# A sparse expert layer in fp32: the two halves of a small place's down sums are added by VectorE, and GpSimd multiplies by the share

## Chip, core and metric

One Trainium2 chip, one of its cores. The metric is the device time of one execution in microseconds (us), as the median of several runs. The engines are TensorE (PE; PEld is its loading of stationary operands), VectorE (DVE), ScalarE (ACT), GpSimd (POOL) and SyncE (SP), which issues the large loads. Matmuls write to PSUM, eight banks of 128 partitions x 512 floats; the other engines read them there.

## What is computed

A residual block: three token mixers (differential attention, an mLSTM, cross-attention), and then a sparse expert network. The change lies in the last:

```python
top_v, top_i = lax.top_k(logits, TOP_K)          # 512 tokens, 32 experts, top 4
h = lax.ragged_dot(xs, w_gate_up, group_sizes) + b_gate_up[e_sorted]
gate, up = h[:, :D_FF], h[:, D_FF:]               # D_MODEL = D_FF = 1024
a = (up + 1.0) * (gate * jax.nn.sigmoid(SWIGLU_ALPHA * gate))   # both clamped
y = lax.ragged_dot(a, w_down, group_sizes) + b_down[e_sorted]
y = y * top_w.reshape(-1)[order][:, None]         # the token's share
out = jax.ops.segment_sum(y, tok, num_segments=T)
```

All in float32. The kernel reaches that precision by splitting operands in two rounded parts, hi and lo, and adding the products hi·hi, hi·lo and lo·hi.

## The kernel before

**Places.** The experts are sorted by their number of tokens and seated in 32 places, 0 to 31. Places 0, 2, 4, ..., 30 and 31 are large (up to 128 tokens), places 1, 3, ..., 29 are small (up to 64, `NS`). The expert part, `stage_moe`, handles place 0, then 15 pairs (`PAIRS`) of a small and a large place in a hardware loop (the last pair is written out again behind it), then place 31. A pass over one place is a `turn`; an odd turn is `turn(..., cur=1, prev=0)`, an even one `turn(..., cur=0, prev=1)`.

**Units.** The weights of an expert come in 12 units of 1 MB: 0 to 3 and 8 to 11 are gate and up, 4 to 7 are down. SyncE loads a unit again as soon as TensorE has used the last one in its place (`s_use`). ScalarE copies it to a rounded hi (`hi`, line 2213, moe_hi, a ring of 6), VectorE subtracts to get lo (`lo`, line 2220, moe_lo), and TensorE multiplies. These two are the splits. ScalarE runs 5 units ahead of TensorE, VectorE 4; the position in a turn is called a slot, 0 to 11, and each engine's queue is an order written out by hand, slot by slot.

**A turn.** TensorE's turn n multiplies tokens of place n with the units 0 to 3 (banks Hb), turns the activations of place n-1 (`turn_a`, line 2306), multiplies those of place n-1 with the down units 4 to 7 (banks Yb[0] and Yb[1]), turns the first half of the activations of n, goes on with the units 8 and 9, transposes the tokens of place n+1 (`turn_x`, line 2248) into the same two banks Yb, and ends with the units 10 and 11. VectorE makes the activations (`swiglu`, lines 2363 and 2369) and the lo parts of activations (`keep_a_lo`, lines 2385 and 2388) and tokens (`keep_x_lo`, lines 2343 and 2345); ScalarE the hi parts (`keep_a_hi`, line 2378, moe_aTh).

**Small places.** In a small place the stationary operand has the hi parts of 64 tokens in columns 0 to 63 and their lo parts in columns 64 to 127, so that two matmuls do for three (lines 2230 and 2231). The result stands in two halves of a bank, partitions 0 to 63 and 64 to 127, that must be added. For this ScalarE copies the bank to SBUF (`to_fold`, line 2278, moe_fold), and TensorE multiplies it with the 128 x 64 matrix `onto`, two identities one above the other, back to partitions 0 to 63 of the bank (`fold_down`, line 2272; one such fp32 matmul is two records). A small place takes six folds: four for gate and up, two for its down sums, Yb[0] and Yb[1], which fall into the even turn.

**The result y.** ScalarE multiplies each half of y (512 columns) by the token's share and writes it to SBUF (`weigh`, line 2399, moe_y). The second half lets two others go on: `turn_x` of TensorE waits for `s_ys` before it overwrites the banks, and GpSimd adds the rows of y to the output with an indirect DMA (`late`, line 2435). GpSimd's queue holds per turn: the gather of the tokens of place n+1 (`fetch`, line 2414), the bias row of n+1, and `late` for place n-1, which first copies the list of tokens and shares to moe_LS (line 2404).

```python
if not (isinstance(n, int) and n < 2):
    pe.wait_ge(s_ys, n * 2 - 2)          # in turn_x
```

Of the kernel before, what the change touches and what calls it, by code (L numbers as in the profile page):

```python
# [27 lines left out]
F32 = mybir.dt.float32  # L28
# [7 lines left out]
P = 128  # L36
# [2103 lines left out]
def stage_moe(K, ctx):  # L2140
# [15 lines left out]
    LS, LO_list = (sb(n, [P, 4], I32) for n in ("LS", "LO"))  # L2156
    Hb, Yb, Tb = K.banks[0:4], K.banks[4:6], K.banks[6:8]
    (s_hi, s_lo, s_use, s_LS, s_XT, s_XTh, s_XTl, s_sel, s_sg, s_cl, s_a, s_aT, s_aTh, s_aTl,
     s_ys, s_sc, s_LO, s_bd, s_h1, s_fk, s_fd, s_fc) = (K.sem("moe_" + n) for n in (
         "unit_hi", "unit_lo", "unit_used", "list_late", "XT", "XT_hi", "XT_lo", "bias_row",  # L2160
         "silu", "up_clipped", "a", "aT", "aT_hi", "aT_lo", "y", "scattered", "over_list", "bias_down", "h1", "to_fold", "folded", "fold_const"))
    CAPPED = ALPHA * LIMIT / (1.0 + math.exp(-ALPHA * LIMIT))
    DOWN = range(4, 8)
    B = 12 * NE + 4
# [103 lines left out]
    def fold_down(pe, f, bank):  # L2268

        pe.wait_ge(s_fc, 1)  # L2270
        pe.wait_ge(s_fk, f + 1)
        nc.tensor.matmul(bank[0:NS, :], onto[:], fold[:], start=True, stop=True).then_inc(s_fd, 1)  # L2272

    def to_fold(act, f, bank, ready):

        act.wait_ge(s_use, ready)
        act.wait_ge(s_fd, f + 1)
        nc.scalar.activation(fold[:], bank[:], ACT.Copy).then_inc(s_fk, 1)
# [109 lines left out]
        nc.vector.scalar_tensor_tensor(aTl[:, cols], Tb[half][:], 1.0 / ALPHA, aTh[:, cols].bitcast(F32), ALU.mult,  # L2388
                                       ALU.subtract).then_inc(s_aTl, 1)

    def weigh(act, n, j, ready, small=0):

        act.wait_ge(s_fd if small else s_use, ready)
        rows = NS if small else P
        if j == (1 if isinstance(n, int) and n == NE - 1 else 0):
            act.wait_ge(s_LS, n + 1)
            if not (isinstance(n, int) and n == 0):
                act.wait_ge(s_sc, n * 16)
        nc.scalar.activation(y[0:rows, j * 512:(j + 1) * 512], Yb[j][0:rows, :], ACT.Copy,  # L2399
                             scale=LS[:].bitcast(F32)[0:rows, 2:3]).then_inc(s_ys, 1)  # L2400

    def entry(pool, dst, kept, n, entries):

# [21 lines left out]
            return  # L2425
        nc.gpsimd.tensor_copy(sel[par][:], K.moe_pick[:, ds(e, 1)].broadcast_to([P, P])).then_inc(s_sel, 1)

    def late(pool, n, entries, small=0):

        rows = NS if small else P  # L2430
        if not (isinstance(n, int) and n == 0):
            hold(K, pool, s_sc, n * 16)
        entry(pool, LS, s_LS, n, entries)
        hold(K, pool, s_ys, n * 2 + 2)
        nc.gpsimd.indirect_dma_start(A["out"], bass.IndirectOffsetOnAxis(ap=LS[0:rows, 0:1], axis=0), y[0:rows, :], None,  # L2435
                                     bounds_check=S - 1, oob_is_err=False, compute_op=ALU.add).then_inc(s_sc, 16)

# [8 lines left out]

    def pair(it, turn, last=0):

        turn(it * 2 + 1, 1, True, 1, 0, 0, it * 6)
        turn(it * 2 + 2, 0, True, 0, 1, 1 - last, None, it * 6)  # L2450

    with nc.Block(no_gpsimd_drain=True) as block:
        @block.sync
# [28 lines left out]

        @block.tensor
        def _(pe):
            def turn(n, par, more, cur=0, prev=0, nxt=0, f=None, g=None):
# [24 lines left out]
                if cur:  # L2510
                    fold_down(pe, f + 1, Hb[1])
                pe.wait_ge(s_aTl, START + n * 2)
                downs(5)
                downs(6)
                if prev:
                    fold_down(pe, g + 4, Yb[0])
                downs(7)
                turn_a(pe, n, 0)
                ups(2, 0)
                if prev:  # L2520
                    fold_down(pe, g + 5, Yb[1])
# [41 lines left out]
        def _(act):  # L2563
# [7 lines left out]
                else:  # L2571
                    hi(act, n + 1, slot - 7)

            def turn(n, par, more, cur=0, prev=0, nxt=0, f=None, g=None):
                for slot in range(12):
                    if slot == 0 and prev:
                        to_fold(act, g + 3, Hb[3], n * 12)
# [9 lines left out]
                        to_fold(act, f + 1, Hb[1], count(n, 3))  # L2587
                    if prev:
                        if slot == 6:
                            to_fold(act, g + 4, Yb[0], count(n, 5))  # L2590
                        if slot == 7:
                            weigh(act, n - 1, 0, g + 6, 1)
                        if slot == 8:
                            to_fold(act, g + 5, Yb[1], count(n, 7))
                        if slot == 9:
                            weigh(act, n - 1, 1, g + 7, 1)
                    else:
                        if slot == 6:
# [61 lines left out]
        def _(pool):  # L2660
# [11 lines left out]
            def turn(n, par, more, cur=0, prev=0, nxt=0, f=None, g=None):  # L2672
# [5 lines left out]
                late(pool, n - 1, listed(expert(pool, n - 1)), prev)  # L2678

            def list_over():  # L2680

# [38 lines left out]
        def _(dve):  # L2720
# [4 lines left out]
                else:  # L2725
                    lo(dve, n + 1, slot - 8)

            def turn(n, par, more, cur=0, prev=0, nxt=0, f=None, g=None):
                for slot in range(12):
                    if slot == (1 if prev else 0):  # L2730
                        swiglu(dve, n - 1, 1, g + 5 if prev else n * 12, prev)
                    if slot == (3 if prev else 2):
                        keep_a_lo(dve, n - 1, 1, prev)
                    if slot == (6 if cur else 4):
                        swiglu(dve, n, 0, f + 3 if cur else count(n, 3), cur)
                    if slot == 8:
# [241 lines left out]
```

## Time and profile before

| | us |
|---|---|
| median of 3 runs | 2204.12 (2203.06 to 2205.08) |
| the profiled execution | 2202.52 |
| its span, first to last instruction | 2200.9 |
| of it the expert part, from the first moe split | from about 1082 on |
| TensorE busy | 2137.9 (97%) |
| VectorE busy | 1562.1 (71%) |
| ScalarE busy | 1323.6 (60%) |
| GpSimd busy | 400.3 (18%) |

All numbers of a view come from one profiled execution; times in it run from the start of its span. Busy shares are means over the span. In the timeline a row is an instruction or a run of the same instruction; "idle before" is how long its engine had nothing to do, with the instruction that ended the wait. The ends of matmuls are modelled and overlap the next start, so the distance between starts is what a matmul costs.

### The profile page before, as it was taken

The numbers are of one execution on the slowest core, as the hardware profiler recorded it, in microseconds if no ns is written. First come the engines' busy times: TensorE is split into PE (matmuls) and PEld (weight loads), VectorE is DVE, ScalarE is ACT, GpSimd is POOL, SyncE is SP. The second block draws the span as 40 slices with busy tenths as digits, with TensorE's granted clock in tenths as the row PEclk, the third lists the DMA queues.
The fourth block names the chain that finished last, engine by engine and source line by source line (L and its number), as shares of the span: only waits on it lengthen the run. The fifth ranks groups of instructions, "written<-read, shape, count | busy, mean of one in ns | idle before, by whom it ended". The sixth has DMA issues, their size and how long they took to land.

```text
span 2200.9 us, 29939 instructions
## 1 busy us (share of the span) xinstructions
PE 2137.9 (97%) x9668; PEld 1656.9 (75%) x9668; DVE 1562.1 (71%) x1706; ACT 1323.6 (60%) x1618; POOL 400.3 (18%) x414
## 2 busy tenths in 40 slices
PE   6999899999999999999799999999999999999998
PEld 6888677776676888888567777777777777777776
DVE  6777444754434334335689999999999999999986
ACT  5565443443323433223268888888888888888884
POOL 3333100201221000001112213212122121121210
PEclk9999999999999999999689999999999999999999
DMA  4110332421112344334579999999999999999993
GB/s 191 58 57 29 102 113 73 145 64 39 38 48 97 95 136 139 97 96 158 210 303 380 390 391 382 396 388 378 396 385 386 392 382 392 380 384 397 382 382 122
DMA packets 87143, 515.76 MB, mean 234 GB/s; under 512 B 13236, under 2 KB 14260, under 8 KB 36312
## 3 DMA queue, kind: packets, MB, share of 16 engines
q1 hardware_dynamic: 79496, 498.06, 59.2%
q0 software_dynamic: 7296, 16.79, 3.4%
q8 instruction: 37, 0.61, 0.1%
q14 instruction: 26, 0.21, 0.0%
q10 hardware_dynamic: 288, 0.09, 0.0%
HBM read 504.66 MB, written 19.40 MB: 238 GB/s over the span
## 4 chain that ended last, share of the span: by engine, by line
PE 50%; DVE 1%; ACT 0%; issue 0%; POOL 0%; POOLq 0%; DVEq 0%; ACTq 0%
PE bank L2237 9%; PE bank L2239 8%; PE bank L2238 8%; PE bank L2230 8%; PE bank L2231 7%; PE bank L2272 4%; PE bank L2259 1%; PE bank L2248 1%; PE bank L2306 1%; PE bank L2290 0%; DVE moe_lo L2220 0%; ACT moe_hi L2213 0%; POOL out L2435 0%; DVE moe_a L2369 0%; DVE moe_um L2363 0%
## 5 line engine op out<-in xcount | busy, mean ns | idle before, releaser
L2220 DVE TENSOR_TENSOR moe_lo<-moe_raw,moe_hi 128x2048 fp32r<-128x2048 f32 x382 | 855.5, 2285 | 11.0 <-ACT moe_hi L2213 9.4
L2213 ACT ACTIVATE moe_hi<-moe_raw 128x2048 fp32r<-128x2048 f32 x380 | 723.5, 1914 | 73.7 <-PE bank L2239 65.8
L173 ACT ACTIVATE unit_hi<-unit_raw 128x1024 fp32r<-128x1024 f32 x116 | 122.2, 1060 | 238.5 <-DMA unit_raw<-in_w_units 232.4
L179 DVE TENSOR_TENSOR unit_lo<-unit_raw,unit_hi 128x1024 fp32r<-128x1024 f32 x116 | 146.5, 1268 | 160.9 <-ACT unit_hi L173 160.5
L2435 POOL DMA_INDIRECT out<-moe_y,moe_LS x32 | 109.8, 3431 | 684.8 <-ACT moe_y L2399 684.8
L2237 PE MATMUL bank<-moe_hi,moe_XTh 128*128 128x512 f32 x544 | 218.9, 402 | 0.0
L2239 PE MATMUL bank<-moe_hi,moe_XTl 128*128 128x512 f32 x544 | 214.3, 394 | 0.0
L2238 PE MATMUL bank<-moe_lo,moe_XTh 128*128 128x512 f32 x544 | 214.0, 393 | 0.0
L2230 PE MATMUL bank<-moe_hi,moe_XTh 128*128 128x512 f32 x480 | 193.3, 403 | 0.0
L2231 PE MATMUL bank<-moe_lo,moe_XTh 128*128 128x512 f32 x480 | 189.8, 395 | 0.0
L2237 PEld LDWEIGHTS bank<-moe_hi,moe_XTh 128*128 128x128 f32 x544 | 103.4, 190 | 43.9 <-issue 24.3
L2230 PEld LDWEIGHTS bank<-moe_hi,moe_XTh 128*128 128x128 f32 x480 | 90.7, 189 | 42.9 <-issue 23.5
L2239 PEld LDWEIGHTS bank<-moe_hi,moe_XTl 128*128 128x128 f32 x544 | 103.0, 189 | 23.1
L2238 PEld LDWEIGHTS bank<-moe_lo,moe_XTh 128*128 128x128 f32 x544 | 103.1, 190 | 21.2
L2237 PE MATMUL bank<-moe_hi,moe_aTh 128*128 128x512 f32 x272 | 107.8, 396 | 0.6 <-DVE moe_lo L2220 0.6
L2239 PE MATMUL bank<-moe_hi,moe_aTl 128*128 128x512 f32 x272 | 106.1, 390 | 0.0
L2238 PE MATMUL bank<-moe_lo,moe_aTh 128*128 128x512 f32 x272 | 105.9, 389 | 0.0
L2231 PEld LDWEIGHTS bank<-moe_lo,moe_XTh 128*128 128x128 f32 x480 | 90.4, 188 | 20.5
L1741 PE MATMUL bank<-yH,unit_hi 128*128 128x512 f32 x256 | 99.8, 390 | 2.2 <-DVE mix_da_lo L1640 2.2
L1743 PE MATMUL bank<-yH,unit_lo 128*128 128x512 f32 x256 | 99.9, 390 | 0.0
L393 PE MATMUL bank<-da_slab_hi,xnH 128*128 128x384 f32 x256 | 92.3, 361 | 5.0 <-DVE xnL L214 5.0
L2272 PE MATMUL bank<-moe_fold,moe_onto 128*64 128x512 f32 x180 | 96.5, 618 | 0.0
(395 smaller groups left out, 4349.5 us busy)
## 6 DMA issues: line engine op xcount, KB each, us to landing
moe_raw<-in_w_moe SPq DMA_DIRECT2D x384, 1024.0 KB, 7.6
unit_raw<-in_w_units SPq DMA_DIRECT2D x116, 512.0 KB, 3.6
da_slab<-in_w_qkv SPq DMA_DIRECT2D x8, 1536.0 KB, 6.6
y_caT<-in_x SPq DMA_DIRECT2D x4, 512.0 KB, 6.1
yda_d<-y_daT SPq DMA_DIRECT2D x1, 2048.0 KB, 6.3
y_daT<-in_blocks_qk SPq DMA_DIRECT2D x1, 2048.0 KB, 10.5
y_daT<-yda_d SPq DMA_DIRECT2D x1, 2048.0 KB, 8.1
y_daT<-in_x SPq DMA_DIRECT2D x1, 2048.0 KB, 8.6
```

The source lines that it names most:

```text
L173: K.nc.scalar.activation(K.whi[:, i, :], K.wraw[:, i, :], ACT.Copy).then_inc(K.s_whi, 1)
L179: K.nc.vector.tensor_tensor(K.wlo[:, i, :], K.wraw[:, i, :], K.whi[:, i, :].bitcast(F32), ALU.subtract).then_inc(K.s_wlo, 1)
L1743: mm = nc.tensor.matmul(bank[:], wl, hi[:, x], start=False, stop=(k0 + k == depth - 1))
L2213: nc.scalar.activation(HI[ring(n, pos)][:], RAW[pos][:], ACT.Copy).then_inc(s_hi, 1)
L2220: nc.vector.tensor_tensor(LO[pos][:], RAW[pos][:], HI[ring(n, pos)][:].bitcast(F32), ALU.subtract).then_inc(s_lo, 1)
L2230: nc.tensor.matmul(bank[:], xh[:, x], HI[ring][:, w], start=start and k == 0, stop=False)
L2231: mm = nc.tensor.matmul(bank[:], xh[:, x], LO[pos][:, w], start=False, stop=stop and k == 3)
L2237: nc.tensor.matmul(bank[:], xh[:, x], HI[ring][:, w], start=start and k == 0, stop=False)
L2238: nc.tensor.matmul(bank[:], xh[:, x], LO[pos][:, w], start=False, stop=False)
L2239: mm = nc.tensor.matmul(bank[:], xl[:, x], HI[ring][:, w], start=False, stop=stop and k == 3)
L2272: nc.tensor.matmul(bank[0:NS, :], onto[:], fold[:], start=True, stop=True).then_inc(s_fd, 1)
L2435: nc.gpsimd.indirect_dma_start(A["out"], bass.IndirectOffsetOnAxis(ap=LS[0:rows, 0:1], axis=0), y[0:rows, :], None, bounds_check=S - 1, oo ...
```

## The change

The folds of the two down sums go. For a small place ScalarE now copies only the lower half of the bank, partitions 64 to 127, to partitions 0 to 63 of y (`keep_rest`, slots 6 and 8 of the even turn). VectorE adds the upper half out of PSUM (`add_rest`, slots 7 and 9, ahead of that slot's split). GpSimd multiplies the whole of y, 64 x 1024, by the share before its indirect DMA. The semaphore `s_ys`, for which `turn_x` waits, is now raised by VectorE for a small place. Large places are as before. In a pair four folds remain; the counts of folds in the loop go from `it * 6` to `it * 4`.

```diff
+    def keep_rest(act, n, j, ready):
+
+        act.wait_ge(s_use, ready)
+        if j == 0:
+            act.wait_ge(s_sc, n * 16)
+        nc.scalar.activation(y[0:NS, j * 512:(j + 1) * 512], Yb[j][NS:P, :], ACT.Copy).then_inc(s_yt, 1)
+
+    def add_rest(dve, j, kept):
+
+        dve.wait_ge(s_yt, kept)
+        cols = y[0:NS, j * 512:(j + 1) * 512]
+        nc.vector.tensor_tensor(cols, Yb[j][0:NS, :], cols, ALU.add).then_inc(s_ys, 1)
...
         entry(pool, LS, s_LS, n, entries)
         hold(K, pool, s_ys, n * 2 + 2)
+        if small:
+            nc.gpsimd.tensor_scalar(y[0:NS, :], y[0:NS, :], LS[0:NS, 2:3].bitcast(F32), None, ALU.mult).then_inc(s_yw, 1)
+            hold(K, pool, s_yw, w)
...
                 downs(5)
                 downs(6)
-                if prev:
-                    fold_down(pe, g + 4, Yb[0])
                 downs(7)
                 turn_a(pe, n, 0)
                 ups(2, 0)
-                if prev:
-                    fold_down(pe, g + 5, Yb[1])
                 ups(2, 1)
...
                     if prev:
                         if slot == 6:
-                            to_fold(act, g + 4, Yb[0], count(n, 5))
-                        if slot == 7:
-                            weigh(act, n - 1, 0, g + 6, 1)
+                            keep_rest(act, n - 1, 0, count(n, 5))
                         if slot == 8:
-                            to_fold(act, g + 5, Yb[1], count(n, 7))
-                        if slot == 9:
-                            weigh(act, n - 1, 1, g + 7, 1)
+                            keep_rest(act, n - 1, 1, count(n, 7))
...
+                    if slot == 7 and prev:
+                        add_rest(dve, 0, it * 2 + 1)
                     if slot == 8:
                         keep_a_lo(dve, n, 0, cur)
+                    if slot == 9 and prev:
+                        add_rest(dve, 1, it * 2 + 2)
```

VectorE in the even turn, from the split of unit 10 to the lo parts of the next place's tokens, in the kernel before:

```order
L2220 TENSOR_TENSOR moe_lo_5680<-moe_raw_5668,moe_hi_5686 128x2048
L2219 REGISTER_ALU
L2220 TENSOR_TENSOR moe_lo_5681<-moe_raw_5669,moe_hi_5687 128x2048
L2388 SCALAR_TENSOR_TENSOR moe_aTl<-bank,moe_aTh 128x512
L2219 ISA
L2220 TENSOR_TENSOR moe_lo_5670<-moe_raw_5658,moe_hi_5682 128x2048
L2219 REGISTER_ALU
L2220 TENSOR_TENSOR moe_lo_5671<-moe_raw_5659,moe_hi_5683 128x2048
L2339 REGISTER_ALU
L2343 TENSOR_TENSOR moe_XTh_8208<-bank,moe_XTh_8208 128x4x64 x2
```

and in the changed one:

```order
L2220 TENSOR_TENSOR moe_lo_5680<-moe_raw_5668,moe_hi_5686 128x2048
L2402 TENSOR_TENSOR moe_y<-bank,moe_y 64x512
L2219 REGISTER_ALU
L2220 TENSOR_TENSOR moe_lo_5681<-moe_raw_5669,moe_hi_5687 128x2048
L2388 SCALAR_TENSOR_TENSOR moe_aTl<-bank,moe_aTh 128x512
L2219 ISA
L2220 TENSOR_TENSOR moe_lo_5670<-moe_raw_5658,moe_hi_5682 128x2048
L2402 TENSOR_TENSOR moe_y<-bank,moe_y 64x512
L2219 REGISTER_ALU
L2220 TENSOR_TENSOR moe_lo_5671<-moe_raw_5659,moe_hi_5683 128x2048
L2339 REGISTER_ALU
L2343 TENSOR_TENSOR moe_XTh_8208<-bank,moe_XTh_8208 128x4x64 x2
```

The second addition stands behind the split of the next place's unit 0 (moe_lo_5670) and ahead of that of unit 1.

TensorE in the same turn, at the first of the two folds, between the down units 6 and 7 (the difference, - before, + changed):

```order
 L2230 MATMUL bank<-moe_hi_5682,moe_aTh 128x512
 L2231 MATMUL bank<-moe_lo_5676,moe_aTh 128x512
-L2271 REGISTER_ALU
-L2272 MATMUL bank<-moe_fold,moe_onto 64x512
 L2225 REGISTER_ALU
 L2230 MATMUL bank<-moe_hi_5683,moe_aTh 128x512
```

The matmuls of units 6 and 7 now follow each other; nothing else moves on TensorE.

## Rows read from the trace of the kernel before

**Rows 1.** The page, busy time of an engine, share of the span, instructions

```profile
PE 2137.9 (97%) x9668; PEld 1656.9 (75%) x9668; DVE 1562.1 (71%) x1706; ACT 1323.6 (60%) x1618; POOL 400.3 (18%) x414
```

**Rows 2.** Window of one pair: PE, PEld, DVE, ACT, POOL busy; clock, DMA share, GB/s

```profile
1562.62:1630.29 67.67, 67.67 (x295) 50.47 (x293) 62.24 (x41) 55.77 (x47) 14.62 (x12) 1.00 1.00 389
```

**Rows 3.** Timeline of TensorE at the first removed fold: start, length, line, operation

```profile
1586.81 0.39 PE L2231 MATMUL bank<-moe_lo,moe_aTh 128*128 128x512 f32 x1
1587.13 1.07 PE L2272 MATMUL bank<-moe_fold,moe_onto 128*64 128x512 f32 x2
1588.13 0.50 PE L2230 MATMUL bank<-moe_hi,moe_aTh 128*128 128x512 f32 x1
```

**Rows 4.** Timeline of TensorE: transposes of a, and of the next tokens

```profile
1578.39 0.60 PE L2306 MATMUL bank<-ident,moe_a 128*128 128x128 f32 x4
...
1597.25 0.39 PE L2239 MATMUL bank<-moe_hi,moe_XTl 128*128 128x512 f32 x1
...
1597.48 1.03 PE L2248 MATMUL bank<-ident,moe_Xg 128*128 128x128 f32 x8
```

**Rows 5.** Timeline of VectorE, same turn, and one row of the next; idle in brackets

```profile
1572.67 0.68 DVE L2363 TENSOR_SCALAR moe_um<-bank 64x512 f32<-64x512 f32 x1
...
1580.80 0.42 DVE L2385 SCALAR_TENSOR_TENSOR moe_aTh<-bank,moe_aTh 128x256 fp32r<-128x256 f32 x1 [2.33 <-ACT moe_aTh L2378]
...
1583.34 0.69 DVE L2363 TENSOR_SCALAR moe_um<-bank 128x512 f32<-128x512 f32 x1
...
1584.67 8.89 DVE L2220 TENSOR_TENSOR moe_lo<-moe_raw,moe_hi 128x2048 fp32r<-128x2048 f32 x4
...
1593.48 0.68 DVE L2388 SCALAR_TENSOR_TENSOR moe_aTl<-bank,moe_aTh 128x512 fp32r<-128x512 f32 x1
...
1594.08 4.48 DVE L2220 TENSOR_TENSOR moe_lo<-moe_raw,moe_hi 128x2048 fp32r<-128x2048 f32 x2
...
1599.32 0.76 DVE L2343 TENSOR_TENSOR moe_XTh<-bank,moe_XTh 128x256 fp32r<-128x256 f32 x2 [0.76 <-ACT moe_XTh L2333]
...
1626.92 0.42 DVE L2385 SCALAR_TENSOR_TENSOR moe_aTh<-bank,moe_aTh 128x256 fp32r<-128x256 f32 x1 [1.54 <-ACT moe_aTh L2378]
```

**Rows 6.** Timeline of ScalarE in the same turn

```profile
1578.59 1.92 ACT L2213 ACTIVATE moe_hi<-moe_raw 128x2048 fp32r<-128x2048 f32 x1 [0.47 <-PE bank L2239]
...
1580.40 0.37 ACT L2378 ACTIVATE moe_aTh<-bank 128x256 fp32r<-128x256 f32 x1
...
1594.72 0.69 ACT L2399 ACTIVATE moe_y<-bank,moe_LS 64x512 f32<-64x512 f32 x1 [1.23 <-PE bank L2272]
```

**Rows 7.** Timelines of TensorE and VectorE at two restarts, and windows around them

```profile
696.14 0.47 PE L1741 MATMUL bank<-yH,unit_hi 128*128 128x512 f32 x1 [2.16 <-DVE mix_da_lo L1640]
696.44 0.39 PE L1742 MATMUL bank<-mix_da_lo,unit_hi 128*128 128x512 f32 x1
...
1132.11 0.69 DVE L2369 SCALAR_TENSOR_TENSOR moe_a<-moe_sg,moe_um 128x512 f32<-128x512 f32 x1
1132.86 1.12 PE L2306 MATMUL bank<-ident,moe_a 128*128 128x128 f32 x4 [3.15 <-DVE moe_a L2369]
...
694.00:700.00 6.00, 3.86 (x17) 3.22 (x18) 4.70 (x8) 5.34 (x9) 0.00 (x0) 1.00 0.31 87
1133.00:1137.00 4.00, 4.00 (x14) 3.06 (x14) 4.00 (x2) 3.52 (x4) 0.00 (x0) 0.62 0.69 283
```

**Rows 8.** Lines and DMA: durations ns min/median/max, and us from issue to landing

```profile
L285 POOL TENSOR_SCALAR ropeS<-ropeS x2: 305/305/305, 19.1 to 21.2; 128x128 f32<-128x128 f32 x2
...
L2404 POOL COPY moe_LS<-first x32: 184/414/5111, 1127.1 to 2176.7; 128x4 int32 x32
...
L2220 DVE TENSOR_TENSOR moe_lo<-moe_raw,moe_hi x348: 2275/2284/2376, 1159.9 to 2137.7; 128x2048 fp32r<-128x2048 f32 x174
...
moe_Xg<-hn_d,moe_LG POOLq DMA_INDIRECT x26, 10.4
```

**Rows 9.** Window with the lowest DMA share of six; columns as in rows 2

```profile
1586.00:1588.00 2.00, 2.00 (x8) 0.85 (x6) 2.00 (x2) 1.90 (x2) 0.00 (x0) 1.00 0.82 332
```

More of the change, by code:

```diff
@@ L2158, in stage_moe @@
     (s_hi, s_lo, s_use, s_LS, s_XT, s_XTh, s_XTl, s_sel, s_sg, s_cl, s_a, s_aT, s_aTh, s_aTl,
-     s_ys, s_sc, s_LO, s_bd, s_h1, s_fk, s_fd, s_fc) = (K.sem("moe_" + n) for n in (
+     s_ys, s_sc, s_LO, s_bd, s_h1, s_fk, s_fd, s_fc, s_yt, s_yw) = (K.sem("moe_" + n) for n in (
          "unit_hi", "unit_lo", "unit_used", "list_late", "XT", "XT_hi", "XT_lo", "bias_row",
-         "silu", "up_clipped", "a", "aT", "aT_hi", "aT_lo", "y", "scattered", "over_list", "bias_down", "h1", "to_fold", "folded", "fold_const"))
+         "silu", "up_clipped", "a", "aT", "aT_hi", "aT_lo", "y", "scattered", "over_list", "bias_down", "h1", "to_fold", "folded", "fold_const", "y_rest", "y_weighed"))
     CAPPED = ALPHA * LIMIT / (1.0 + math.exp(-ALPHA * LIMIT))
@@ L2389, in keep_a_lo, with weigh @@
                                        ALU.subtract).then_inc(s_aTl, 1)
-    def weigh(act, n, j, ready, small=0):
-        act.wait_ge(s_fd if small else s_use, ready)
-        rows = NS if small else P
+    def keep_rest(act, n, j, ready):
[7 more added lines that the diff above has]
+        nc.vector.tensor_tensor(cols, Yb[j][0:NS, :], cols, ALU.add).then_inc(s_ys, 1)
+    def weigh(act, n, j, ready):
+        act.wait_ge(s_use, ready)
         if j == (1 if isinstance(n, int) and n == NE - 1 else 0):
@@ L2398, in weigh @@
                 act.wait_ge(s_sc, n * 16)
-        nc.scalar.activation(y[0:rows, j * 512:(j + 1) * 512], Yb[j][0:rows, :], ACT.Copy,
-                             scale=LS[:].bitcast(F32)[0:rows, 2:3]).then_inc(s_ys, 1)
+        nc.scalar.activation(y[:, j * 512:(j + 1) * 512], Yb[j][:], ACT.Copy,
+                             scale=LS[:].bitcast(F32)[:, 2:3]).then_inc(s_ys, 1)
     def entry(pool, dst, kept, n, entries):
@@ L2426, in bias_row, with late @@
         nc.gpsimd.tensor_copy(sel[par][:], K.moe_pick[:, ds(e, 1)].broadcast_to([P, P])).then_inc(s_sel, 1)
-    def late(pool, n, entries, small=0):
+    def late(pool, n, entries, small=0, w=None):
         rows = NS if small else P
@@ L2447, in pair @@
     def pair(it, turn, last=0):
-        turn(it * 2 + 1, 1, True, 1, 0, 0, it * 6)
-        turn(it * 2 + 2, 0, True, 0, 1, 1 - last, None, it * 6)
+        turn(it * 2 + 1, 1, True, 1, 0, 0, it * 4)
+        turn(it * 2 + 2, 0, True, 0, 1, 1 - last, None, it * 4, it)
     with nc.Block(no_gpsimd_drain=True) as block:
@@ L2484, in _, with turn @@
         def _(pe):
-            def turn(n, par, more, cur=0, prev=0, nxt=0, f=None, g=None):
+            def turn(n, par, more, cur=0, prev=0, nxt=0, f=None, g=None, it=None):
                 def ups(j, half):
@@ L2572, in ahead, with turn @@
                     hi(act, n + 1, slot - 7)
-            def turn(n, par, more, cur=0, prev=0, nxt=0, f=None, g=None):
+            def turn(n, par, more, cur=0, prev=0, nxt=0, f=None, g=None, it=None):
                 for slot in range(12):
@@ L2670, in _, with turn @@
             nc.gpsimd.tensor_tensor(onto[:], K.ident[:, 0:NS], K.ident[:, NS:P], ALU.add).then_inc(s_fc, 1)
-            def turn(n, par, more, cur=0, prev=0, nxt=0, f=None, g=None):
+            def turn(n, par, more, cur=0, prev=0, nxt=0, f=None, g=None, it=None):
                 if more:
@@ L2677, in turn @@
                     bias_row(pool, n + 1, 1 - par, e, n * 12, nxt)
-                late(pool, n - 1, listed(expert(pool, n - 1)), prev)
+                late(pool, n - 1, listed(expert(pool, n - 1)), prev, it + 1 if prev else None)
             def list_over():
@@ L2726, in ahead, with turn @@
                     lo(dve, n + 1, slot - 8)
-            def turn(n, par, more, cur=0, prev=0, nxt=0, f=None, g=None):
+            def turn(n, par, more, cur=0, prev=0, nxt=0, f=None, g=None, it=None):
                 for slot in range(12):
```

## Prediction, made before the changed kernel ran

> **What bounds the kernel now.** I read the page first, for its busy shares: TensorE is busy for 97% of the span [rows 1]. A share is an average over stages, so the next view is the table of windows, cut to one period of the loop over pairs of places, in the expert part where the change lies. There TensorE is busy for 67.67 of 67.67 us, VectorE for 62.24, ScalarE for 55.77, and the DMA engines are at a share of 1.00 [rows 2]. The loop runs 15 times (1,015 of the 2,200.9 us), and the periods I measured differ by 0.01 us. So three resources stand within 8% of one another and TensorE is the one that never rests. What TensorE sheds is a gain only if nobody else is late where TensorE then arrives. Hence the third view: the timelines of TensorE, VectorE and ScalarE through one turn for a large place, laid over one another [rows 3 to 6].
>
> **What is removed.** A fold stands between two matmuls that start 1.32 us apart, 1586.81 and 1588.13 [rows 3]; two neighbours without one start 0.23 us apart [rows 4]. A fold costs 1.09 us of TensorE. Two of six go in each of 15 pairs: 30 × 1.09 = 32.7 us, the most that the change can give. ScalarE loses two copies and two weighings per pair and gets two copies of half height. It waited before its second weighing in this turn (1.23 us [rows 6]), so its saving is worth nothing by itself.
>
> **What is added on VectorE.** Two additions of 64 x 512 with one operand in PSUM. The nearest rows: the correction of the activations from PSUM starts at 1593.48 and the next operation at 1594.08, so such an operation shifts what follows by 0.60 us; it takes 0.68 us itself. A 64-row operation takes 0.68 us, a 128-row one 0.69 us: half height is not cheaper [rows 5]. I take 0.60 us of queue and 0.69 us to the end, with 0.1 us either way. That is 1.2 us more on an engine with 5.4 us of rest per period [rows 2]; by totals it fits. What decides is where its rest lies.
>
> **The wait that is new in kind.** TensorE's transposes of the next place's tokens go into the two banks in which the down sums stood, and wait until both halves of y are made. Before, ScalarE made them: the second from 1594.72 to 1595.41 [rows 6], and the transposes began at 1597.48 with no idle time before them [rows 4]. Now VectorE makes the second half, and its addition stands in VectorE's queue behind the splitting of the next place's unit 0. When does VectorE come there?
>
> Walk back along its queue to its last rest [rows 5]. At 1580.80 it had idled 2.33 us for ScalarE's aTh, 1580.40 to 1580.77. That stands behind a split which ScalarE began at 1578.59 when TensorE freed a ring place [rows 6]; the transposes of a, which it also needs, are at 1578.39 [rows 4]. Both are ahead of either removed fold (1587.13 and the next 6.5 us later). Nothing that is removed lets VectorE leave 1580.80 earlier, relative to TensorE's work ahead of the folds. From there it runs without rest until 1598.56: one split, two swiglu operations, four splits, the correction, two splits. The four splits take 8.89 us with 2.28 for the last, so one starts 2.20 us after another. The split of unit 0 starts at 1594.08. The first addition pushes that to 1594.68; the second addition starts at 1594.68 + 2.20 = 1596.88 and ends at 1597.57.
>
> Now TensorE. Its last matmul ahead of the transposes starts at 1597.25 and is moved forward by two folds, 2.18 us, to 1595.07; it ends at 1595.46. It then stands still for VectorE. From the end of a VectorE operation to the matmul that waited for it there are 0.06 us (1132.11 + 0.69 to 1132.86 [rows 7]): the transposes start at 1597.63, after 2.17 us of idle time. That is 0.15 us *later* than the 1597.48 of before. A matmul after such a rest costs a little more: 0.30 us to the next one instead of 0.23 [rows 7, 4], so 0.07 to 0.14 us more. **Per pair: 0.15 + 0.10 = 0.25 us longer,** since TensorE does the same as before from the transposes to the next 1578.39. Fifteen pairs: **+3.8 us**. Both ends: an addition of 0.1 us less gives +0.1 us per pair or +1.5 us in all; 0.1 us more per addition, and the dearer restart, give +0.5 us per pair or +7.5 us. The saving of 32.7 us is there, but as idle time of TensorE.
>
> **What is added on GpSimd.** One multiplication of 64 x 1024 in SBUF ahead of the scatter. No row shows one. The nearest is a tensor_scalar of 128 x 128 at 0.305 us [rows 8]; eight times as many elements are at most 2.4 us. GpSimd also gets in late: the copy of four numbers per partition takes between 0.18 and 5.11 us [rows 8]. So the scatter goes out 2 us (the later y) plus 1 to 7 us later. Behind it in GpSimd's queue stand the gather of tokens for the place after next and its bias row. TensorE transposes those tokens at the end of the next turn, some 30 us on, and a gather lands in 10.4 us [rows 8]: I cost this at nothing; the upper end is rival D.
> The Trainium skill, GPSIMD Engine Reference, section 8 (Key points), speaks against this edit: GpSimd shares its SBUF interfaces with VectorE, and contends with VectorE instructions that have two SBUF inputs. The splits are such instructions. This trace agrees on one side only: GpSimd's copies are stretched, while 348 splits lie between 2.275 and 2.376 us [rows 8]. By the rule the multiplication may also delay a split; by the rows it is GpSimd that yields.
>
> **The transfers.** With the loop 0.25 us longer they see no change: 24 loads per period, share 1.00.
>
> **Rivals.**
> *A. The adds cancel the folds (my forecast):* 2204.12 + 3.8 = 2207.9 us. Chance 0.66. Within it I give 0.47 to a change of 0.2% or less (4.4 us, about what a measurement of this kernel can tell from none) and 0.19 to more.
> *B. The stall costs TensorE its clock.* It becomes the only idle time of the loop, 2.17 us of it. For: after 3.15 us of idle time at 1132.86 the window 1133 to 1137 shows a granted clock of 0.62 of full speed [rows 7]. Against: after 2.16 us at 696.14, between dense matmuls as here, the window shows 1.00 [rows 7]. Price: a mean of 0.62 over 4 us is 3.0 us at 1.2 GHz instead of 2.4, in which half the work is lost, 1.5 us a time; in all 15 pairs 22 us, hence 2207.9 + 22 = 2230 us, and 2219 in half of them. It decides from an idle time somewhere between 2.16 and 3.15 us. Chance 0.15. The Trainium skill, TensorE: Matmul & The Clock Gate, "HAM oscillation", describes this very pattern, a gap in every step of a loop that brings half rate back each time.
> *C. VectorE comes in time.* If its place were set by TensorE's progress behind the folds, the loop would shrink by up to 2.18 us: 2171.4 us by TensorE alone. For: VectorE has 5.4 us of rest per period. Against: the rest lies at 1580.80, ahead of the additions, and nothing removed stands ahead of it. Then the DMA engines would be late next: the lowest share that I found in windows of 2 us is 0.82, from 1586 to 1588 [rows 9], 0.36 us of rest. With 0.4 to 1 us of rest per period the gain would be 6 to 15 us and whatever lead the loads have over their use: 2171 to 2198 us, I take 2185. Chance 0.11.
> *D. GpSimd holds VectorE up (slower).* The multiplication begins when the second addition is done, in the middle of splits. The additions leave VectorE 1.2 us later, TensorE 0.25. It has rests of 0.76, 1.54 and 2.33 us ahead of the next additions [rows 5]; only when GpSimd takes more than about 3.5 us from it per pair do the additions come later still. 1 us beyond that is 15 us: 2223 us. Chance 0.08.
>
> **How the numbers follow.** The profiled execution was 2202.52 us (span 2200.9), within 1.6 us of the median of 2204.12; forecast on its scale 2206.3, on the median's 2207.9. Range 2202 to 2224: A whole but for its tails (0.63), half of B (0.09), D (0.08). Left out are C and B in nearly every pair. Faster by over 0.2%: 0.11 (C). Within: 0.47. Slower: 0.19 + 0.15 + 0.08 = 0.42.
>
> **What would show it.** In the profile after: folds down from 90 to 60; a new wait of TensorE's transposes for VectorE's moe_y, 15 times at about 2.2 us, some 33 us in all; a period near 67.9 us; TensorE busy about 65.5 of it; granted clock 1.00 (B: below); GpSimd's multiplication 1 to 3 us, behind splits that stay at 2.28 us (D: stretched, or VectorE idle). I am wrong if VectorE's wait at the place of 1580.80 is gone, if the transposes wait under 1.5 us, or if ScalarE or a load is named there.

## The result, and the profile after

| | before | changed |
|---|---|---|
| median, range (7 runs each) | 2204.12 (2202.87 to 2208.07) | 2212.66 (2210.77 to 2213.82) |
| ratio, 95% interval | | 1.0038 [1.0027, 1.0049] |
| span of the profiled execution | 2200.9 | 2211.1 |

The change costs 8.5 us: slower by more than 0.2%, 4.8 us above the forecast and inside its range. The class to which the forecast gave most, a change of 0.2% or less (0.47), did not come; slower had 0.42. In the two profiled executions the spans differ by 10.2 us, of which 1.3 stand ahead of the loop's first stall, in a part that the change does not touch. TensorE did get lighter, and the time came back as a wait. (Its busy time fell by 25.5 us and not by the 36.8 of the wait, in part because work at the lower clock, shown below, takes longer.) The page, row of the engines' busy time (before: [rows 1]):

```profile
PE 2112.4 (96%) x9608; PEld 1659.9 (75%) x9608; DVE 1581.8 (72%) x1736; ACT 1304.5 (59%) x1588; POOL 519.8 (24%) x429
```

Waits of TensorE from 1160 us on: what waited for what, us in total, times, the longest. The first row has no counterpart before.

```profile
PE bank L2248 <- DVE moe_y L2402: 36.8, 15, 2.6
PE bank L2237 <- DVE moe_lo L2220: 0.6, 1, 0.6
```

The timeline of TensorE and VectorE at one of the 15 places (start, length, idle time before in brackets). VectorE first, as in [rows 5]:

```profile
1586.11 0.42 DVE L2385 SCALAR_TENSOR_TENSOR moe_aTh<-bank,moe_aTh 128x256 fp32r<-128x256 f32 x1 [2.33 <-ACT moe_aTh L2378]
...
1596.58 0.68 DVE L2402 TENSOR_TENSOR moe_y<-bank,moe_y 64x512 f32<-64x512 f32 x1
...
1599.99 2.27 DVE L2220 TENSOR_TENSOR moe_lo<-moe_raw,moe_hi 128x2048 fp32r<-128x2048 f32 x1
1602.18 0.68 DVE L2402 TENSOR_TENSOR moe_y<-bank,moe_y 64x512 f32<-64x512 f32 x1
```

And TensorE, as in [rows 4]:

```profile
1600.09 0.39 PE L2239 MATMUL bank<-moe_hi,moe_XTl 128*128 128x512 f32 x1
1602.92 1.09 PE L2248 MATMUL bank<-ident,moe_Xg 128*128 128x128 f32 x8 [2.44 <-DVE moe_y L2402]
```

VectorE's last rest before both additions is still the one of 2.33 us, with the same length and the same releaser as before. From it, everything goes in a row; the second addition ends at 1602.86 and the transposes of the next tokens begin 0.06 us later. From the rest to those transposes it was 1597.48 − 1580.80 = 16.68 us before and is 16.81 us now.

So the ordinary period grew by 0.15 us, from 67.67 [rows 2] to 67.82. But four of the 15 are longer by 1.5 to 1.6 us. Windows of an ordinary period, of a long one, and of 4 us from the stall of each kind (start and end, length, busy time of PE, PEld, DVE, ACT and POOL, granted clock, DMA share, GB/s):

```profile
1397.85:1465.67 67.82, 65.38 (x288) 50.16 (x289) 63.62 (x43) 54.52 (x44) 23.14 (x12) 1.00 1.00 388
1533.49:1602.92 69.43, 66.99 (x289) 51.53 (x289) 63.57 (x43) 54.52 (x44) 20.84 (x12) 0.98 0.98 381
1602.00:1606.00 4.00, 3.08 (x18) 2.71 (x19) 4.00 (x6) 1.87 (x3) 2.92 (x1) 1.00 1.01 422
1533.00:1537.00 4.00, 3.51 (x13) 3.18 (x14) 3.37 (x5) 1.42 (x3) 3.35 (x1) 0.57 1.01 424
```

Two equal stalls (times in which TensorE has nothing to do) of 2.44 us, one followed by TensorE at 2.4 GHz and one by a granted clock of 0.57, which is most of that stretch at 1.2 GHz. In the timeline of TensorE after the second:

```profile
1533.49 1.97 PE L2248 MATMUL bank<-ident,moe_Xg 128*128 128x128 f32 x8 [2.44 <-DVE moe_y L2402]
...
1535.68 0.63 PE L2237 MATMUL bank<-moe_hi,moe_XTh 128*128 128x512 f32 x1
...
1536.88 0.39 PE L2237 MATMUL bank<-moe_hi,moe_XTh 128*128 128x512 f32 x1
```

The eight transposes take 1.97 us, not 1.09, and the matmuls 0.63, not 0.39, until 1536.9: 3.4 us. The sum closes: 15 × 0.15 + 4 × 1.55 = 8.4 us, where 8.5 were measured. Of these only 2.2 us are the later addition; 6.2 are the clock. The four are the pairs 2, 6, 9 and 13; in two further kernels with the same stall (e6 and e10) it is four of 15 as well, the pairs 3, 6, 10 and 14, and 3, 6, 10 and 13. What picks them is open: the length of the stall does not.

GpSimd's multiplication, 15 times (duration in ns: shortest, median, longest; first and last start):

```profile
L2448 POOL TENSOR_SCALAR moe_y<-moe_y,moe_LS x15: 4707/4709/4711, 1193.1 to 2148.8; 64x1024 f32<-64x1024 f32 x15
```

### The profile page after: what moved, and what is told of

Its sections match the earlier page's. It is cut to its first block, busy times and chain, and to the rows that moved or that the text cites. A ratio compares the mean times of both kernels' runs of the same rounds, so it can differ in the third digit from the quotient of the medians.

```text
span 2211.1 us, 29775 instructions
## 1 busy us (share of the span) xinstructions
PE 2112.4 (96%) x9608; PEld 1659.9 (75%) x9608; DVE 1581.8 (72%) x1736; ACT 1304.5 (59%) x1588; POOL 519.8 (24%) x429
## 4 chain that ended last, share of the span: by engine, by line
PE 37%; DVE 9%; issue 4%; ACT 0%; DVEq 0%; POOL 0%; ACTq 0%; POOLq 0%
DVE moe_lo L2220 7%; PE bank L2237 7%; PE bank L2238 6%; PE bank L2239 6%; PE bank L2230 5%; PE bank L2231 5%; PE bank L2272 3%; PE bank L2248 2%; PE bank L2259 1%; PE bank L2306 1%; DVE moe_y L2402 1%; DVE moe_um L2363 1%; DVE moe_aTl L2388 0%; PE bank L2290 0%; ACT moe_aTh L2378 0%
## 5 line engine op out<-in xcount | busy, mean ns | idle before, releaser
L2450 POOL DMA_INDIRECT out<-moe_y,moe_LS x32 | 104.4, 3261 | 249.2 <-ACT moe_y L2411 235.6
L2448 POOL TENSOR_SCALAR moe_y<-moe_y,moe_LS 64x1024 f32<-64x1024 f32 x15 | 70.6, 4709 | 364.8 <-DVE moe_y L2402 364.8
```

## The experiments

Three questions: does the second addition's place in VectorE's queue set TensorE's start, as the forecast says; does the stall cost the clock in some pairs; and does GpSimd take anything from VectorE? The median of before was 2204.4 for e1 to e4, 2204.9 for e5 to e8, and 2206.0 for e9 and e10, each group on one chip.

### e1: the second addition one split earlier

```diff
-                    if slot == 9 and prev:
+                    if slot == 8 and prev:
                         add_rest(dve, 1, it * 2 + 2)
```

> The changed kernel with the second addition moved in VectorE's queue from slot 9 to slot 8, ahead of the split of the next place's unit 0 instead of behind it. Theory (the place of this addition in VectorE's queue ends the wait): the addition ends 2.2 us earlier relative to TensorE, the wait of the transposes falls from 2.44 us to about 0.3 us, the clock holds in all pairs, and the pair takes 67.82 - 2.1 = 65.7 us; 2212.7 - 15 x 2.1 - 4 x 1.5 = about 2175 us. Rival DMA (24 loads per pair already keep the DMA engines at a share of 1.00): TensorE's wait goes, but loads land later and later and ScalarE and TensorE come to wait for moe_raw; the pair does not go below about 67 us on the mean: 2190 to 2200 us. Rival GpSimd (the multiplication of 4.7 us holds VectorE up): less than half of the wait goes, 2200 us or more.

Measured: 2182.33 us (2179.26 to 2185.02), ratio 0.9901 [0.9888, 0.9915]. The period is 66.12 us, not the 65.7 expected. Moving one operation of 0.6 us by one split of 2.2 us is worth 30 us against the changed kernel. The waits of TensorE from 1160 us on:

```profile
PE bank L2248 <- DVE moe_y L2402: 3.7, 15, 0.4
PE bank L2306 <- DVE moe_a L2369: 3.3, 14, 0.2
```

The old wait is down to 0.24 us in 14 of 15 places and 0.39 in the last, and a second one has come up: TensorE's transposes of moe_a in the odd turn, for VectorE.

### e2: both additions in slot 7

```diff
                     if slot == 7 and prev:
                         add_rest(dve, 0, it * 2 + 1)
+                        add_rest(dve, 1, it * 2 + 2)
...
-                    if slot == 9 and prev:
-                        add_rest(dve, 1, it * 2 + 2)
```

> The changed kernel with both additions together in slot 7 of VectorE's queue, ahead of the split of unit 11. Theory: the second addition ends at about the start of what is now unit 11's split, 2 us before TensorE arrives; no wait at the transposes at all, the pair takes 65.4 us and the kernel about 2171 us, 4 us less than with slot 8. Rival DMA: as with slot 8, 2190 to 2200 us, and the two places of the addition give the same time.

Measured: 2179.29 us (2178.68 to 2181.06), ratio 0.9885 [0.987, 0.99], and a period of 66.10 us, not the 65.4 expected. The wait for moe_y is gone altogether, but the other has taken its place:

```profile
PE bank L2306 <- DVE moe_a L2369: 9.7, 14, 0.7
```

TensorE is still not alone on the path. e7 to e9 follow this up.

### e3: no sum and no multiplication

The lower halves of the small places' down sums are left out, ScalarE weighs the upper half, and GpSimd's multiplication goes.

```diff
...
-        nc.scalar.activation(y[0:NS, j * 512:(j + 1) * 512], Yb[j][NS:P, :], ACT.Copy).then_inc(s_yt, 1)
+        nc.scalar.activation(y[0:NS, j * 512:(j + 1) * 512], Yb[j][0:NS, :], ACT.Copy,
+                             scale=LS[:].bitcast(F32)[0:NS, 2:3]).then_inc(s_ys, 1)
...
-            nc.gpsimd.tensor_scalar(y[0:NS, :], y[0:NS, :], LS[0:NS, 2:3].bitcast(F32), None, ALU.mult).then_inc(s_yw, 1)
...
-                        add_rest(dve, 0, it * 2 + 1)
...
-                        add_rest(dve, 1, it * 2 + 2)
```

> The changed kernel without the two additions and without GpSimd's multiplication: ScalarE weighs partitions 0 to 63 of the down sums as they stand, and the lower halves of the down sums of small places are left out of the result. It shows what the two folds are worth alone. Theory: folds 1.2 us each, 30 of them, 36 us less than before: 2168 us, TensorE busy in all of a pair of 65.3 us. Rival DMA: 2190 to 2200 us, with waits for loads.

Measured: 2172.11 us (2171.12 to 2173.84), ratio 0.9853 [0.9838, 0.9868]. One window, and the loads issued between 1900 and 2100 us (count, size, median us from issue to landing):

```profile
1574.67:1639.87 65.20, 65.20 (x289) 50.24 (x288) 62.07 (x41) 54.51 (x45) 14.98 (x11) 1.00 1.01 400
```

```profile
moe_raw<-in_w_moe SPq DMA_DIRECT2D x74, 1024.0 KB, 17.9
```

With TensorE alone on the path a period is 65.20 us, so a fold is worth (67.67 − 65.20) / 2 = 1.23 us. The loads landed 7.7 us after their issue before and 17.9 us here, between 1900 and 2100 us: the transfers no longer keep up, but the first eleven periods are 65.20 us all the same, and only the last three are longer (65.4 to 66.2 us).

### e4: the stall filled with unread matmuls

Eight matmuls into a bank that nobody reads then, ahead of the even turn's transposes; the rest is the changed kernel.

```diff
+                if prev:
+                    for _ in range(8):
+                        nc.tensor.matmul(Tb[1][:], sel[par][:], K.moe_bias[:, 0:HF], start=True, stop=True)
```

> The changed kernel with eight matmuls of 128x512 whose result nobody reads, put on TensorE's queue ahead of the transposes of the even turn; 8 x 0.23 = 1.8 us, less than the wait of 2.44 us there. Theory (VectorE sets the start of the transposes, and the clock fell in 4 of 15 pairs because TensorE stood still): the pairs stay at 67.82 us, the wait shows as 0.6 us, the clock falls nowhere in the loop, and the time is 2204.1 + 15 x 0.15 = 2206.4 us, 6 us faster than the changed kernel in spite of more work. Rival (the fall of the clock has nothing to do with the wait, or the wait is TensorE's own cost): 2212.7 us or more, up to 2212.7 + 27 us.

Measured: 2208.06 us (2205.11 to 2210.1), ratio 1.0014 [1.0005, 1.0024]. Every period is 67.81 to 67.87 us (the last 68.02); the long ones are gone. Timeline of TensorE:

```profile
1601.67 1.09 PE L2248 MATMUL bank<-ident,moe_Xg 128*128 128x128 f32 x8 [0.57 <-DVE moe_y L2402]
```

Some 1.9 us of extra work per pair costs no time, and the kernel is 4.6 us *faster* for it (1.7 us above what was expected of it). That shows both halves of the sum: TensorE's work does not set the period, and it is the stall that brings the falls of the clock, since they go with it.

### e5: the second addition one split later

```diff
-                    if slot == 9 and prev:
-                        add_rest(dve, 1, it * 2 + 2)
                     if slot == 10:
+                        if prev:
+                            add_rest(dve, 1, it * 2 + 2)
```

(It stands ahead of the correction of the next tokens in that slot.)

> The changed kernel with VectorE's second addition one split later still (slot 10 in place of slot 9); nothing is left out. The split takes 2.20 us of the queue, so TensorE should stand idle 2.44 + 2.20 = 4.64 us ahead of the even turn's transposes. Theory (the place in VectorE's queue sets the start, and a stall this long halves the clock every time): the ordinary period goes from 67.82 to 70.0 us, and the fall of the clock adds the 1.5 us that four of fifteen pairs showed, in each pair now: 71.5 us, 15 x (71.5 - 67.67) = 57 us over the kernel before, about 2262 us. Rival (the idle time costs itself alone, and the four long pairs of the changed kernel have another cause): 70.0 us a pair, 15 x 2.35 = 35 us over, about 2240 us. If something other than VectorE's addition opened the wait, nothing moves: 2212 to 2213 us.

Measured: 2264.57 us (2264.47 to 2268.27), ratio 1.0276 [1.0261, 1.0291]; all periods are 71.66 to 71.73 us. The timeline at one stall, and the window of 4 us from there:

```profile
1697.32 1.69 PE L2248 MATMUL bank<-ident,moe_Xg 128*128 128x128 f32 x8 [4.64 <-DVE moe_y L2402]
```

```profile
1697.00:1701.00 4.00, 3.69 (x14) 3.21 (x15) 1.45 (x4) 1.88 (x3) 2.85 (x1) 0.58 0.61 252
```

The idle time is 4.64 us, as the queue's arithmetic gave, and now the clock falls every time: 71.69 = 67.82 + 2.20 + 1.67.

This run also shows GpSimd's multiplication without VectorE beside it. It starts when the second addition is done, and here VectorE then rests for over 2 us. GpSimd's line, and at the last of the 15 places the multiplication and VectorE's next operation:

```profile
L2448 POOL TENSOR_SCALAR moe_y<-moe_y,moe_LS x15: 2845/2846/2857, 1195.7 to 2199.4; 64x1024 f32<-64x1024 f32 x15
...
2199.38 2.85 POOL L2448 TENSOR_SCALAR moe_y<-moe_y,moe_LS 64x1024 f32<-64x1024 f32 x1 [27.00 <-DVE moe_y L2402]
...
2202.33 1.29 DVE L2345 TENSOR_TENSOR moe_XTl<-bank,moe_XTh 128x512 fp32r<-128x512 f32 x2 [3.17 <-ACT moe_XTh L2335]
```

Alone it takes 2.85 us.

### e6: the changed kernel without the multiplication

```diff
-            nc.gpsimd.tensor_scalar(y[0:NS, :], y[0:NS, :], LS[0:NS, 2:3].bitcast(F32), None, ALU.mult).then_inc(s_yw, 1)
-            hold(K, pool, s_yw, w)
```

> The changed kernel without GpSimd's multiplication: the share is left out of the small places, so their outputs are not weighed. Theory (VectorE's queue alone sets the loss; GpSimd's 4.71 us lie beside everything): 2212 to 2213 us, an ordinary period of 67.82 us, and the clock falls in a few of the fifteen pairs as before. Rival (GpSimd's multiplication holds VectorE up, as the splits of 4.74 us beside it in place of 4.49 hint): the two splits beside it are 0.25 us shorter; if they are on the way to TensorE's next start, 15 x 0.25 = 3.8 us less, about 2209 us.

Measured: 2212.54 us (2210.7 to 2217.75), ratio 1.0037 [1.0024, 1.0051], which is the changed kernel's own. The two splits beside the multiplication did change, 4.74 us to 4.47. VectorE's timeline in the changed kernel, and in e6:

```profile
1605.65 4.74 DVE L2220 TENSOR_TENSOR moe_lo<-moe_raw,moe_hi 128x2048 fp32r<-128x2048 f32 x2
```

```profile
1606.56 4.47 DVE L2220 TENSOR_TENSOR moe_lo<-moe_raw,moe_hi 128x2048 fp32r<-128x2048 f32 x2
```

So GpSimd does take 0.27 us from VectorE, and all of it from one operation: in the changed kernel the first of the two splits takes 2.54 us, in e6 2.27.

```profile
1605.65 2.54 DVE L2220 TENSOR_TENSOR moe_lo<-moe_raw,moe_hi 128x2048 fp32r<-128x2048 f32 x1
```

```profile
1606.56 2.27 DVE L2220 TENSOR_TENSOR moe_lo<-moe_raw,moe_hi 128x2048 fp32r<-128x2048 f32 x1
```

It comes behind the additions, and VectorE's next rest takes it up: 1.08 us there, 1.35 in e6.

```profile
1632.42 0.42 DVE L2385 SCALAR_TENSOR_TENSOR moe_aTh<-bank,moe_aTh 128x256 fp32r<-128x256 f32 x1 [1.08 <-ACT moe_aTh L2378]
```

```profile
1633.33 0.42 DVE L2385 SCALAR_TENSOR_TENSOR moe_aTh<-bank,moe_aTh 128x256 fp32r<-128x256 f32 x1 [1.35 <-ACT moe_aTh L2378]
```

### e7: e2 without the multiplication

The edit of e6 on the kernel of e2.

> The kernel of e2_adds_slot7 (both additions in slot 7) without GpSimd's multiplication: the share is left out of the small places. In e2 the multiplication took 14.8 us, ran across the odd turn's first activation on VectorE, and that operation took 0.89 us where it takes 0.69 without a multiplication (e3_no_sum); TensorE waited 0.69 us for its result. Theory (two additions of 0.60 us in VectorE's queue make most of that wait, the multiplication 0.20 us of it): a wait of 0.5 us, a period of 65.9 us in place of 66.10, 15 x 0.2 = 3 us under e2, 2176 us. Rival 1 (the multiplication makes the whole wait): no wait, 65.2 to 65.4 us a pair, 2166 to 2173 us. Rival 2 (it makes none of it): 66.1 us a pair, 2179 us.

Measured: 2177.21 us (2176.93 to 2179.24), ratio 0.9877 [0.9863, 0.9891]; a period of 65.91 us. In e2 the multiplication takes 14.8 us, and the activation beside it is longer. e2's multiplication, then from its timelines VectorE's operation and TensorE's wait:

```profile
L2448 POOL TENSOR_SCALAR moe_y<-moe_y,moe_LS x15: 14778/14781/15230, 1189.8 to 2115.3; 64x1024 f32<-64x1024 f32 x15
```

```profile
1599.06 0.89 DVE L2369 SCALAR_TENSOR_TENSOR moe_a<-moe_sg,moe_um 128x512 f32<-128x512 f32 x1
1600.01 0.66 PE L2306 MATMUL bank<-ident,moe_a 128*128 128x128 f32 x4 [0.69 <-DVE moe_a L2369]
```

The same two in e7:

```profile
1596.82 0.69 DVE L2369 SCALAR_TENSOR_TENSOR moe_a<-moe_sg,moe_um 128x512 f32<-128x512 f32 x1
1597.57 0.66 PE L2306 MATMUL bank<-ident,moe_a 128*128 128x128 f32 x4 [0.49 <-DVE moe_a L2369]
```

0.20 us of activation, 0.20 of wait, 0.19 of period: here the multiplication costs what it takes from VectorE, some 3 us in 15 pairs by the periods. (The medians of e2 and e7 differ by 2.1 us, and their intervals overlap.) The other 0.49 us is VectorE's queue.

### e8: the share without GpSimd

A version that computes everything: ScalarE multiplies the lower half while it copies it, VectorE the upper one while it adds. Both additions stand in slot 7, as in e2, and GpSimd's multiplication goes.

```diff
...
+        nc.scalar.activation(y[0:NS, j * 512:(j + 1) * 512], Yb[j][NS:P, :], ACT.Copy,
+                             scale=LS[:].bitcast(F32)[0:NS, 2:3]).then_inc(s_yt, 1)
...
-        nc.vector.tensor_tensor(cols, Yb[j][0:NS, :], cols, ALU.add).then_inc(s_ys, 1)
+        nc.vector.scalar_tensor_tensor(cols, Yb[j][0:NS, :], LS[0:NS, 2:3].bitcast(F32), cols, ALU.mult, ALU.add).then_inc(s_ys, 1)
```

> A version that computes everything and has neither the folds nor GpSimd's multiplication: both additions in slot 7, ScalarE multiplies the lower half by the share while it copies it, and VectorE multiplies the upper half by the share in the same operation that adds. Theory: such an operation from a PSUM bank takes no longer than the addition (the form with a scale is 0.68 us on the turned activations too, 64 rows or 128), so the time is that of e7_slot7_no_multiply: 2176 us, a wait of TensorE for the odd turn's activation of 0.5 us. Rival 1 (the share's pointer makes the operations longer, as an operation with both inputs in SBUF took 0.69 to 0.89): 0.1 to 0.2 us more for each of two, 2179 to 2182 us. Rival 2 (the multiplication on GpSimd was the whole wait): 2166 to 2173 us.

Measured: 2177.13 us (2176.64 to 2177.94), ratio 0.9875 [0.9861, 0.9889]; a period of 66.03 us and a wait of 0.61 us. The operation with the share is 0.06 us longer than the plain addition (0.73 against 0.67 us), twice per pair, and that is the 0.12 us by which wait and period exceed those of e7. The theory's time held; it had put the operation with the share at no longer than the addition, which was 0.06 us too low.

### e9: the odd turn's activation one split earlier

The kernel of e8, and VectorE makes moe_a of the place ahead one split earlier.

```diff
-                    if slot == (1 if prev else 0):
-                        swiglu(dve, n - 1, 1, g + 5 if prev else n * 12, prev)
+                    if slot == 1 and prev:
+                        swiglu(dve, n - 1, 1, g + 5, prev)
+                    if slot == 11 and prev:
+                        swiglu(dve, n, 1, n * 12 + 12)
...
+            swiglu(dve, 0, 1, 12)
```

> The kernel of e8_share_no_multiply with one move in VectorE's queue: the odd turn's first two operations, which make moe_a of the expert ahead (0.68 + 0.69 us), stand one split of 2.20 us earlier. Their input (the last matmul of the unit ahead) ended at 1591.24 in e8 and they began at 1594.53, so they may begin at 1592.33; moe_a is then there at 1593.7, where TensorE is free for it at 1595.4. Theory (TensorE's only wait in the period is VectorE's place in that queue): the wait of 0.61 us goes, the period is 65.3 to 65.4 us until the loads land late as in e3_no_sum, and the time 2168 to 2173 us. Rival 1 (the split that is now 1.4 us later is waited for by its unit): TensorE waits about as long for moe_lo instead, 66.0 us a pair, 2177 us. Rival 2 (the loads cannot follow a shorter period at all): TensorE or ScalarE waits for DMA from the first pairs on, 65.8 to 66.0 us, 2175 to 2177 us.

Measured: 2172.53 us (2168.31 to 2175.5), ratio 0.9847 [0.983, 0.9865]; against e8 through the runs of before that is about 0.3% less, with intervals that just overlap. Two windows, one early and one late:

```profile
1240.00:1305.20 65.20, 65.20 (x291) 50.24 (x289) 63.11 (x43) 54.72 (x45) 35.97 (x12) 1.00 1.01 401
1895.00:1961.00 66.00, 65.40 (x290) 50.27 (x289) 63.29 (x42) 54.93 (x45) 31.40 (x12) 1.00 1.00 396
```

TensorE's timeline in the late one, and the landing of the loads from 1900 to 2100 us:

```profile
1930.55 1.07 PE L2272 MATMUL bank<-moe_fold,moe_onto 128*64 128x512 f32 x2 [0.40 <-ACT moe_fold L2278]
```

```profile
moe_raw<-in_w_moe SPq DMA_DIRECT2D x73, 1024.0 KB, 17.8
```

The wait for moe_a is gone and the period is 65.20 us for eight pairs: TensorE alone. After that it is about 66.0: ScalarE waits for loads (45.1 us in all), its copies for the remaining folds come later, and TensorE waits for those. That is the limit of the transfers, at 396 to 401 GB/s.

### e10: GpSimd multiplies by a number

```diff
-            nc.gpsimd.tensor_scalar(y[0:NS, :], y[0:NS, :], LS[0:NS, 2:3].bitcast(F32), None, ALU.mult).then_inc(s_yw, 1)
+            nc.gpsimd.tensor_scalar(y[0:NS, :], y[0:NS, :], 0.25, None, ALU.mult).then_inc(s_yw, 1)
```

> The changed kernel with GpSimd multiplying by a number written in the instruction (0.25) and not by the share read from moe_LS: the small places are wrongly weighed. It asks why that multiplication takes 4.71 us (and 12.0 and 14.8 us where it runs beside other work of VectorE in e1 and e2). Theory (it waits for the data side that it has in common with VectorE's splits): it stays at about 4.7 us. Rival (reading the share costs it): it falls to 2.4 us or under, the bound the prediction took. The kernel's time stays at 2212 to 2213 us either way.

Measured: one run, 2215.32 us, where 2212 to 2213 were expected; the kernel before was 1.9 us slower on this chip too, and the pairs are those of the changed kernel, four long ones among them. The multiplication:

```profile
L2448 POOL TENSOR_SCALAR moe_y<-moe_y x15: 4631/4640/4649, 1195.8 to 2151.7; 64x1024 f32<-64x1024 f32 x15
```

Reading the share is 0.07 us of the 4.71. The rival falls. The same instruction takes 2.85 us where VectorE rests beside it (e5), 4.71 in the changed kernel, 12.0 in e1 and 14.8 in e2. So 1.86 of the 4.71 us, and 9 and 12 us in e1 and e2, come with VectorE's work. Which of its operations hold GpSimd up, and why only some, is not shown.

## Why the forecast was right, and where it was off

**The mechanism of A held.** The forecast walked back VectorE's queue to its last rest, found it ahead of both folds, and concluded that the removed 2 × 1.2 us would return as a wait. The rest is where it was, 2.33 us long; TensorE waits there 15 times; the addition ends, and 0.06 us later the transposes begin. e1, e2 and e5 move the addition and the wait follows: to 0.24, to none, to 4.64 us; e4 shows that TensorE's own work no longer counts. But A makes only 2.2 of the 8.5 us.

**The fold was mis-sized, without consequence.** It was priced at 1.32 − 0.23 = 1.09 us from two starts. The matmul behind a fold, 1588.13 in [rows 3], starts its neighbour 0.33 us later as well, not 0.23; TensorE's timeline before:

```profile
1588.46 0.39 PE L2231 MATMUL bank<-moe_lo,moe_aTh 128*128 128x512 f32 x1
```

That makes 1.19 us from the starts, and 1.23 by e3. So the stall was 2.44 us, not 2.17, and the most that the change could give 37 us, not 32.7. On the forecast's path this did not matter, since the period is set from VectorE's rest.

**Restart cost, mis-sized.** It was put at 0.07 to 0.14 us. From the transposes to VectorE's next rest it was 50.99 us before and is 51.01 now: 0.02. From the rest to the transposes the forecast had 0.15 us more, and 0.13 were measured. Hence +0.15 us a pair and not +0.25.

**The step that failed: B as an alternative to A, and the row against it.** The forecast gave the clock's fall 0.15 and its likeliest case none, because a stall of 2.16 us at 696.14 had left the clock at 1.00 [rows 7]; it took the length of the stall to decide whether the clock falls. That row was an exception. The stall stands ahead of the expert part, in code that no run changes, and every other trace has it too, at 2.13 to 2.46 us: in all eleven the clock behind it is 0.57 to 0.59 over 4 us. In the changed kernel, timeline and window (columns as in [rows 2]):

```profile
699.94 0.47 PE L1741 MATMUL bank<-yH,unit_hi 128*128 128x512 f32 x1 [2.29 <-DVE mix_da_lo L1640]
...
699.94:703.94 4.00, 4.00 (x11) 3.18 (x12) 4.00 (x7) 3.98 (x7) 0.00 (x0) 0.57 0.20 80
```

and in e2, where it is shorter than the 2.16 us of the kernel before:

```profile
698.45 0.47 PE L1741 MATMUL bank<-yH,unit_hi 128*128 128x512 f32 x1 [2.13 <-DVE mix_da_lo L1640]
...
698.45:702.45 4.00, 4.00 (x11) 3.15 (x12) 4.00 (x7) 3.98 (x7) 0.00 (x0) 0.57 0.22 86
```

One harmless stall had been read as a harmless length. In the loop the fall came with 2.44 us in 4 of 15 pairs (e6 and e10 the same), with 4.64 us in 15 of 15, with 0.6 us in none. Its price was right: 1.5 us a time forecast, 1.5 to 1.6 measured. B did name a partial case, 2219 us with a fall in half of the pairs, but as an alternative to the forecast and not as a term of its sum; in fact the fall comes on top of A in some pairs: 4 × 1.55 = 6.2 us, less the 1.5 us by which the pair was overpriced (15 × 0.10), is the distance of 4.7 us to the forecast. The pattern is the one which the Trainium skill, TensorE: Matmul & The Clock Gate, "HAM oscillation", describes, a gap in each step of a loop that brings half rate back; there it comes back every time, here only with 4.64 us.

**GpSimd.** The multiplication was estimated at up to 2.4 us, from eight times the elements per partition, and takes 4.71, of which 2.85 are its own (e5). Costed at nothing, it costs nothing in this kernel (e6). Rival D was right that it takes something from VectorE (0.27 us of one split), wrong that it matters at this place; with the additions earlier it does, 0.2 us a pair (e7). The Trainium skill, GPSIMD Engine Reference, section 8 (Key points), has the two engines contend where VectorE reads two inputs from SBUF. These runs agree: the operations that were stretched, one split in the changed kernel and moe_a's in e1 and e2, are both of that kind, and in e5, where no such operation runs beside it, nothing is stretched and the multiplication is at its shortest. The forecast read from its rows that only GpSimd yields; both do, VectorE by 0.20 to 0.27 us in one operation for each multiplication, GpSimd by 1.9 to 12 us.

**Rival C named the right prize.** Its 2171 to 2198 us are where the versions with the additions earlier lie (2182, 2179, 2177, 2173). It was also right that DMA is the next limit, but too early with it: at 66.1 us a pair (e1, e2) loads landed in 9 us and nobody waited for them; at 65.2 the period holds for eight pairs (e9) or eleven (e3) before it grows.

**The best version** is e9, 2172.53 us, 1.5% faster than before with everything computed: the removed folds are worth nearly what they seemed (33.5 us against the kernel before on the same chip, of 37), once VectorE's two additions stand early in its queue, its activation is moved out of their way, and the share rides on operations that run anyway.

## What to carry to other kernels

Work taken from the busiest engine is a gain only if the operation that it waits for next can come earlier too. Walk back in that operation's queue to its engine's last rest and see whether anything removed lies ahead of it; if not, look for a place one slot earlier before giving the change up, since here one place in the queue was worth 30 us and both edits looked the same by busy time. And when a change turns TensorE's work into idle time, price the clock for every such stall: one stall behind which the clock held does not make its length harmless. Look for the same stall in more than one execution, and count on a share of them.

## What the runs showed of the hardware

- TensorE, idle times in the loop and the clock behind them: 0.6 us, never below full (e4, 15 of 15); 2.44 us, down to 1.2 GHz for some 3.4 us in 4 of 15 (the changed kernel, e6 and e10 alike); 4.64 us, in 15 of 15 (e5). One fall costs 1.5 to 1.7 us. A single stall of 2.13 to 2.46 us in the mixers was followed by a fall in eleven traces of twelve, so equal stalls do not give equal clocks.
- A GpSimd multiplication of 64 x 1024 floats in SBUF by one number per partition took 2.85 us beside a resting VectorE, and 4.71, 12.0 or 14.8 us beside a working one, the same to within 0.5 us over 15 executions of a kernel. One of VectorE's operations beside it, with both inputs in SBUF, became mostly 0.20 to 0.27 us longer; in e5, and in five of the changed kernel's 15 pairs, none did.
- A VectorE addition of 64 x 512 with one input in PSUM takes 0.67 us and shifts its queue by 0.60; with a multiplication by a number per partition in the same operation it takes 0.73.
